# Block 1's banded attention: two score banks in place of three, two banks for the turned probabilities in place of one

## The reference, cut to what matters

```
for gi, (window, dilation) in enumerate(SWA_GROUPS):
    o_g, lse_g = dilated_window_attention(sq[:, :, gi], sk[:, :, gi], sv[:, :, gi], window, dilation)
    outs.append(o_g)
    lses.append(lse_g)
alpha = jax.nn.softmax(jnp.stack(lses, axis=0), axis=0)
o_swa = jnp.sum(alpha[..., None] * jnp.stack(outs, axis=0), axis=0).astype(x.dtype)
```

## Time and profile before

| | us |
|---|---|
| median of 3 runs | 2975.48 |
| lowest and highest | 2974.71, 2977.23 |
| the profiled execution | 2973.67 |
| its span, first to last instruction | 2971.9 |
| PE busy in the span | 2885.5 |
| DVE busy | 1452.6 |
| ACT busy | 1088.2 |

### The profile page before, as it was taken

How to read it: one execution, slowest core, us unless ns; L and a number is a source line. 1 busy time by engine, 2 the same in 40 slices (tenths; PEclk the granted TensorE clock), 3 DMA queues, 4 the chain that set the end, 5 groups by cost and what they waited for, 6 DMA issues and landing times.

```text
span 2971.9 us, 36175 instructions
## 1 busy us (share of the span) xinstructions
PE 2885.5 (97%) x13458; PEld 2313.2 (78%) x13458; DVE 1452.6 (49%) x2090; ACT 1088.2 (37%) x1777; POOL 224.1 (8%) x166
## 2 busy tenths in 40 slices
PE   8999999899999999998999999999999999999998
PEld 5698767788788886677788888888886677788886
DVE  5673476544444334555454443544334555454432
ACT  4512343433333224655432222332224655433221
POOL 0000000000100021000120003000121001110011
PEclk9999999999999999999999999999999999999999
DMA  3201211124232323110222232223322111122232
GB/s 118 71 22 47 85 64 54 32 91 138 83 99 92 106 89 107 36 50 30 78 85 95 95 109 89 91 92 99 105 93 85 41 50 43 64 99 92 99 108 77
DMA packets 68364, 238.08 MB, mean 80 GB/s; under 512 B 10272, under 2 KB 12448, under 8 KB 67616
## 3 DMA queue, kind: packets, MB, share of 16 engines
q1 hardware_dynamic: 66240, 227.87, 23.2%
q10 hardware_dynamic: 2016, 8.77, 0.8%
HBM read 234.51 MB, written 2.10 MB: 80 GB/s over the span
## 4 chain that ended last, share of the span: by engine, by line
PE 68%; DVE 3%; ACT 2%; issue 1%; DVEq 0%; ACTq 0%
PE bank L381 19%; PE bank L383 19%; PE bank L382 19%; PE bank L860 3%; PE bank L886 3%; PE bank L665 2%; PE bank L872 2%; PE bank L638 1%; ACT L_probs L936 1%; DVE L_scores L984 1%; PE bank L1518 0%; PE bank L227 0%; PE bank L1461 0%; DVE L_area L1827 0%; ACT L_h_hi L1648 0%
## 5 line engine op out<-in xcount | busy, mean ns | idle before, releaser
L381 PE MATMUL bank<-L_h_hi,L_w_hi 128*128 128x512 f32 x1776 | 702.5, 396 | 6.1 <-DVE residual L1837 3.8
L382 PE MATMUL bank<-L_h_lo,L_w_hi 128*128 128x512 f32 x1776 | 691.1, 389 | 0.0
L383 PE MATMUL bank<-L_h_hi,L_weight_ring_low 128*128 128x512 f32 x1760 | 685.2, 389 | 0.0
L369 ACT CAST L_w_hi<-L_weight_ring 128x1024 fp32r<-128x1024 f32 (+2 forms) x290 | 324.1, 1117 | 906.4 <-PE bank L383 893.4
L375 DVE TENSOR_TENSOR L_weight_ring_low<-L_weight_ring,L_w_hi 128x1024 fp32r<-128x1024 f32 (+2 forms) x290 | 394.1, 1359 | 374.4 <-ACT L_w_hi L369 374.3
L381 PEld LDWEIGHTS bank<-L_h_hi,L_w_hi 128*128 128x128 f32 x1776 | 333.5, 188 | 82.2 <-issue 5.7
L382 PEld LDWEIGHTS bank<-L_h_lo,L_w_hi 128*128 128x128 f32 x1776 | 333.5, 188 | 73.7 <-issue 5.7
L383 PEld LDWEIGHTS bank<-L_h_hi,L_weight_ring_low 128*128 128x128 f32 x1760 | 330.4, 188 | 69.5
L381 PE MATMUL bank<-L_act_hi,L_w_hi 128*128 128x512 f32 x704 | 273.9, 389 | 0.0
L382 PE MATMUL bank<-L_act_lo,L_w_hi 128*128 128x512 f32 x704 | 273.9, 389 | 0.0
L383 PE MATMUL bank<-L_act_hi,L_weight_ring_low 128*128 128x512 f32 x704 | 273.9, 389 | 0.0
(11 more groups left out here) (338 smaller groups left out, 3872.4 us busy)
## 6 DMA issues: line engine op xcount, KB each, us to landing
L_weight_ring<-ffn_in SPq DMA_DIRECT2D x174, 512.0 KB, 3.3
L_weight_ring<-ffn_out SPq DMA_DIRECT2D x64, 704.0 KB, 4.1
B_weight_ring<-w_sqk SPq DMA_DIRECT2D x24, 512.0 KB, 3.3
B_weight_ring<-w_dn SPq DMA_DIRECT2D x16, 512.0 KB, 3.3
B_weight_ring<-w_gate SPq DMA_DIRECT2D x16, 512.0 KB, 3.2
L_weight_ring<-w_sna_qk SPq DMA_DIRECT2D x16, 512.0 KB, 3.3
L_weight_ring<-w_mix_out SPq DMA_DIRECT2D x16, 512.0 KB, 3.3
B_weight_ring<-w_sv SPq DMA_DIRECT2D x12, 512.0 KB, 3.3
```

What stands on the lines that cost most here:

```text
L369: e.copy(hv.high(at)[:, 0:width], hv.raw(sh, at)[:, 0:width]).then_inc(hv.w_hi_done, 1)
L381: e.matmul(out, a_hi, b_hi, start=start, stop=False)
L382: e.matmul(out, a_hi, b_lo, start=False, stop=False)
L383: return e.matmul(out, a_lo, b_hi, start=False, stop=stop)
```

## The change

The scores use banks 5 and 6; bank 7 goes to the turned probabilities, which use banks 3 and 7 in turn. The credits that the engines give at the start follow: `pt_done` two in place of one, `biased` two in place of three. No instruction is added or removed and none changes its place in an engine's list; what changes is which earlier event two kinds of PE instruction wait for.

```
-        at_ = Attn(sc, 1280, [5, 6, 7], [3], [4], big)
+        at_ = Attn(sc, 1280, [5, 6], [3, 7], [4], big)
...
                 e.sem_inc(jb.rstd, 2)
                 e.sem_inc(at_.exped, 2)
-                e.sem_inc(at_.pt_done, 1)
+                e.sem_inc(at_.pt_done, 2)
...
                 e.sem_inc(jb.done, 2)
-                e.sem_inc(at_.biased, 3)
+                e.sem_inc(at_.biased, 2)
```

## The result

The changed kernel takes 3026.55 us (median of 4 runs, 3025.33 to 3030.94) against 2975.72: a ratio of 1.0177, 95% interval 1.0165 to 1.0189, which is 51 us slower. The forecast was 3022, from 3008 to 3034. The kernel before has four runs here, three of them those of the first table. It was measured again beside the experiments, with medians of 2977.02 (the first four experiments) and 2976.51 us (the last four); their ratios are to those, and its own runs spread over some 10 us, so a difference of 1 or 2 us between two kernels says little.

A forecast was written before the change was run, and what follows sets the result against it. The prediction took PE, busy 97% of the span, to bound the kernel. Waits of 34.2 us plus a low clock of 14.4 made 48.6 on 2973.67, given as 3022 us, range 3008 to 3034.

The forecast's parts named there:

- PE's idle time counts in full: Whole kernel: PE is busy 97% of the span, so a wait added ahead of PE is lost unless it replaces another.
- The wait term: Third score segments wait for DVE to read the first: 1.2 + 15.0 + 10.1 + 6.3 + 0 + 1.6 = 34.2 us.
- The lag is DVE's own work and does not shrink: Units 1, 5, 9: DVE's lag begins when the last job's matmuls end and moves with PE; 5.0 us late each.
- The second bank's gain: Transposes: unit 2's 0.88 us already counted; real in units 11 to 15, 0.9 or 1.33 per unit, 0.5 taken back.
- The clock term: Stage: one low clock stretch of some 1.6 us behind each long PE wait, eight units plus unit 15, 14.4 us.
- The rival with two: PE's waits in the stage: the clock pays twice for each, eight more times 1.6 us, 3035 us; chance 0.10.
- the one in which the low level falls into the waits: PE's waits in the stage: the clock costs nothing extra, the waits alone give 3008 us; chance 0.10.
- The price of a short stretch: Low-clock stretch after a PE wait: at half clock, some 1.6 us lost in all.
- The sum: Whole kernel: 34.2 + 14.4 = 48.6 us added to 2973.67 gives 3022.3, given as 3022 us.
- What the profile would show: L860 waiting for L995 some 35 us in about 10 waits; L872 for L947 at most 2 or 3 us.
- The faster rival: Units 1 to 10: DVE reads the first segment before PE asks for the third, giving 2962 us; chance 0.02.

The follow-up runs named there:

- the first four experiments: Half the change alone, 3032.3 us; that with filler matmuls in the waits, 3010.24; maxima ahead of the last job in eight units, with the change 2977.1, without it 2983.65.
- the last four: Maxima placed so no job is late: with the change 2972.24 us, without 2972.29; with the change and the gate's low half later 2970.97; with one turned bank 2981.5.
- the reordered list: The changed kernel with DVE's maxima ahead of the last job in units 1, 2, 3, 5, 6, 7, 9 and 10: 2977.1 us, ratio 1.0001.
- the one with DVE's list placed: The changed kernel with DVE's maxima ahead of the last job in six units, between its two parts in units 3 and 7: 2972.24 us, ratio 0.9986.
- the kernel before with DVE's list placed: The kernel before with DVE's maxima ahead of the last job in six units, between its two parts in units 3 and 7: 2972.29 us, ratio 0.9986.

## Why the prediction was right, point by point

- *PE's idle time counts in full.* Right: 50.2 of the stage's 50.9 us are PE's waits (33.2) and its low clock (17), and nothing behind the stage gave them back.
- *The wait term, 34.2 us.* It measured 33.2 net (46.0 + 0.6 in place of 1.8 + 11.6). By unit, from the second segment's start to the third's, after against before: unit 1 5.35 against 0.43, so 4.9 (I had 5.0); unit 2 5.25 against 1.97, 3.3 (3.4); unit 3 5.24 against 2.19, 3.05 (3.16). Unit 5 is as unit 1. PE started 0.06 us after DVE's end in all of them, where I had taken the 0.15 of the one such wait before. In unit 4 the first score and the third chunk are 3.57 apart where they were 3.60: zero, as put. But the forecast also said that PE would not be idle ahead of the third segment there, and it is, for 1.77 us: the waits of its second and third chunk (1.23 us, and 0.45) have moved to the score.
- *The lag is DVE's own work and does not shrink.* Right: unit 5's wait is 4.76 like unit 1's. That this work is the reason in these units, the reordered list shows: 3026.6 to 2977.1 with no instruction changed.
- *The second bank's gain is inside the figures of units 2 and 3, and is real only in units 11 to 15.* Right: without it the stage takes 4.4 us more, all behind the first score of unit 12, where I had put 4.5 less 0.5. The medians are 5.8 apart.
- *The clock term, 14.4 us.* The step that was mis-sized, though it is close: 17. I had one low stretch for each wait, nine more in all. There were two behind each other in units 5, 6, 7, 9 and 11, one in units 1, 2, 10 and 15, none in unit 3, and a second one in unit 0, where I had put none: thirteen more than before, once the two that the kernel before had in units 8 and 12 are taken off. The rival with two had half of the truth, and so had the one in which the low level falls into the waits: of the 44.5 us that it lasts longer PE works in 37.0. The price of a short stretch in which PE works throughout, 1.6 us, was right (0.47 times 3.4), but the average of the thirteen is 1.3. That the count was too low and the price for each too high, and the sum so near, is luck in part.
- *The sum.* 34.2 + 14.4 against 33.2 + 17 in the stage; 3022 against 3026.55.
- *What the profile would show.* I had named "some 35 us in about 10 waits" of L860 for L995. It is 46.0 in 15. The slip is that a wait that moves from the chunk to the score adds to the score's row without adding time: 35 was the net figure. The sum was not touched by it.
- *The faster rival.* Its condition, that DVE reads the first segment before PE asks for the third, was made true by the reordering. It did not bring 2962 even then, but 2972, for the missing score bank kept 8.6 us of waits, mostly in units 11, 15 and 0, for which that rival set no condition.

## What to carry to other kernels

Count buffers between two engines against the lag of the reader, not against the number of waits in the profile of before: three banks for the scores showed hardly a wait because they covered exactly one unit while DVE finished something else, and taking one away put DVE's 5 us of other work into PE's path. Before giving a buffer to the wait that shows, look at what the next wait behind it would be; the gain of the one is first swallowed there. And where the reader is merely late by its order of work, moving its short, awaited operation ahead of the long one adds no instruction and was worth 50 us here; then see which of its other results has become late, for the same move lost 6.6 us where nothing had waited for it.

## What the runs showed of the hardware that I had not expected

- Idle PE cost about half as much again through its clock in this stage: 33 us of waits brought 17 us. Filling the waits with matmuls that nobody reads made a kernel 22 us faster.
- The clock's answer to a wait is not fixed. In the changed kernel a wait of 3.78 us (unit 3) had no low stretch behind it and one of 3.79 (unit 7) had 6.8 us; those of 4.76 had 3.4 us in unit 1 and 6.8 us in units 5 and 9. Unit 15's wait of 2.50 us had 3.4 us in the changed kernel and none in the one with DVE's list placed. The 1.83 us ahead of unit 12 had 3.4 us in the kernel before, and the same 1.84 us had none in the kernel before with DVE's list placed:

```profile
556.16 1.62 PE L862 MATMUL bank<-B_arena 128*128 128x128 f32 x6 [1.84 <-DVE B_segment_max L997]
...
556.20:560.00 3.80, 3.62 (x17) 2.81 (x18) 2.04 (x12) 1.46 (x2) 0.00 (x0) 1.00 0.00 0
```

A price for one wait is only good as a mean over many.
